# One matmul for the distance biases, split squares, and constant multiplications at the head of a decoder layer

## The reference, cut to what matters

```
mod = silu(c) @ w_ada + b_ada                  # w_ada: 2048 x 18432
sh1, sc1, g1, sh2, sc2, g2, sh3, sc3, g3 = split(mod, 9)
h = rms_norm(x, norm_ffn1) * (1 + sc1) + sh1
x = x + 0.5 * g1 * ((silu(h @ w1_gate) * (h @ w1_up)) @ w1_down)
...
s_w = q @ k * scale + rel_bias[t5_bucket(distance)]    # inside the token mixing
```

## Time and profile before

| | |
|---|---|
| three runs, median | 2060.33 us (2058.78 to 2060.92) |
| the profiled execution | 2060.54 us, its span 2058.7 us |
| TensorE busy | 2024.6 us, 98% of the span |
| VectorE, ScalarE busy | 1398.9 us (68%), 873.7 us (42%) |
| TensorE on the chain that ended last | 93% |
| mean transfer rate | 259 GB/s over the span |

### The profile page before, as it was taken

The page is one execution under the profiler, slowest core; times in us unless marked ns, Lnnn a source line. Parts: engine busy times, 40 slices in busy tenths (PEclk is TensorE's granted clock), DMA queues, the critical chain, the costliest instruction groups (busy, mean ns, idle before and its releaser), DMA issues.

```text
span 2058.7 us, 26899 instructions
## 1 busy us (share of the span) xinstructions
PE 2024.6 (98%) x9331; PEld 1605.0 (78%) x9331; DVE 1398.9 (68%) x1864; ACT 873.7 (42%) x1119; POOL 36.6 (2%) x56
## 2 busy tenths in 40 slices
PE   7999999999999999999999999999999999999998
PEld 4668888788888888787787888788888888888886
DVE  4557887877778889896556669777775545545454
ACT  3344434344443434543444644544444444434333
POOL 0000000000000000000005000000000000000000
PEclk9999999999999999999999999999999999999999
DMA  8998999799989889698967138589986777675654
GB/s 309 387 349 301 332 318 322 261 292 297 278 303 327 308 319 347 221 365 290 290 194 260 42 134 305 165 276 291 295 251 197 197 199 205 198 217 197 199 186 133
DMA packets 343366, 533.10 MB, mean 259 GB/s; under 512 B 80874, under 2 KB 99397, under 8 KB 342377
## 3 DMA queue, kind: packets, MB, share of 16 engines
q1 hardware_dynamic: 342648, 529.90, 77.6%
q10 hardware_dynamic: 624, 1.97, 0.3%
HBM read 520.04 MB, written 3.89 MB: 254 GB/s over the span
## 4 chain that ended last, share of the span: by engine, by line
PE 93%; DVE 2%; issue 1%; DMA 1%; ACT 1%; SPq 0%; ACTq 0%
PE ps L825 29%; PE ps L827 29%; PE ps L826 29%; PE ps L869 1%; PE ps L906 1%; DMA ada_half<-in_w_ada_dram 1%; PE ps L854 1%; DVE ada_acc L1941 1%; DVE w_lo L1923 1%; PE ps L1372 1%; PE ps L1375 1%; PE ps L1402 1%; PE ps L1207 0%; ACT w_hi L1496 0%; DMA raw<-in_w_uq_dram 0%
## 5 line engine op out<-in xcount | busy, mean ns | idle before, releaser
L1496 ACT ACTIVATE w_hi<-raw 128x1024 fp32r<-128x1024 f32 (+1 forms) x657 | 688.9, 1054 | 929.0 <-PE ps L827 552.6
L1923 DVE TENSOR_TENSOR w_lo<-raw,w_hi 128x1024 fp32r<-128x1024 f32 (+1 forms) x657 | 796.0, 1220 | 408.0 <-ACT w_hi L1496 402.4
L825 PE MATMUL ps<-w_hi,hT_hi 128*128 128x512 f32 (+1 forms) x1856 | 741.7, 400 | 6.5 <-DVE hT_lo L2058 4.3
L827 PE MATMUL ps<-w_hi,hT_lo 128*128 128x512 f32 (+1 forms) x1856 | 731.8, 394 | 0.0
L826 PE MATMUL ps<-w_lo,hT_hi 128*128 128x512 f32 (+1 forms) x1856 | 731.7, 394 | 0.0
L825 PEld LDWEIGHTS ps<-w_hi,hT_hi 128*128 128x128 f32 x1856 | 349.8, 188 | 102.4 <-issue 15.3
L827 PEld LDWEIGHTS ps<-w_hi,hT_lo 128*128 128x128 f32 x1856 | 349.8, 188 | 83.6
L826 PEld LDWEIGHTS ps<-w_lo,hT_hi 128*128 128x128 f32 x1856 | 350.1, 189 | 79.8 <-issue 0.5
L1941 DVE SCALAR_TENSOR_TENSOR ada_acc<-ada_raw,silu_c,ada_acc 128x512 f32<-128x512 f32 x420 | 315.4, 751 | 8.1
L825 PE MATMUL ps<-w_hi,actT_hi 128*128 128x512 f32 x704 | 280.0, 398 | 0.0
L827 PE MATMUL ps<-w_hi,actT_lo 128*128 128x512 f32 x704 | 279.1, 396 | 0.0
(11 more groups left out here) (245 smaller groups left out, 947.3 us busy)
## 6 DMA issues: line engine op xcount, KB each, us to landing
ada_raw<-in_w_ada_dram SPq DMA_DIRECT2D x224, 512.0 KB, 5.5
raw<-in_w_gate_dram SPq DMA_DIRECT2D x176, 512.0 KB, 4.9
raw<-in_w_up_dram SPq DMA_DIRECT2D x176, 512.0 KB, 4.9
raw<-in_w_down_dram SPq DMA_DIRECT2D x176, 512.0 KB, 5.0
raw<-in_w_in_dram SPq DMA_DIRECT2D x72, 512.0 KB, 5.8
ada_half<-in_w_ada_dram SPq DMA_DIRECT2D x14, 2048.0 KB, 12.9
raw<-in_w_out_dram SPq DMA_DIRECT2D x32, 512.0 KB, 5.4
actT_lo<-norm_tmp SPq DMA_DIRECT2D x240, 32.0 KB, 3.2
```

The source lines that it names most:

```text
L825: pe.matmul(bank, lhs_hi, rhs_hi, start=start, stop=False)
L827: return pe.matmul(bank, lhs_lo, rhs_hi, start=False, stop=stop)
L1496: act.activation(part(U, w_hi, s), part(U, raw, s), ACT.Copy).then_inc(hi_done, 1)
L1923: dve.tensor_tensor(part(U, w_lo, s), part(U, raw, s), part(U, w_hi, s).bitcast(F32), ALU.subtract)\
```

## The change

It has four parts. The nine bias matmuls become one: the table of 33 x 9 biases itself is the stationary operand, and the result has the nine rows on nine partitions. It runs after `turn_norm` 0, its scaled copy on VectorE after `first_low(0)`; `rel_rep` and its copy on GpSimd are gone. The store to memory now reads each of the nine rows 128 times, so that memory holds what it held before. The squares of `x` tile 1 are made by VectorE (`second_squares`), between the copy of `v_cols` and the mean, while ScalarE makes only those of tile 0; it also runs a Silu on a constant before them. And TensorE runs `keep_busy(n)`: n matmuls of the 128 x 128 tile of ones by itself into bank 0, whose result nothing reads; 28 before the transpose of `v_rows`, then 5, 12 and 6 at three later places.

```diff
--- before.py
+++ after.py
@@ -347,11 +347,12 @@
             bucket_sb = sb("bucket_sb", [BUCKETS + 1, 384], within=s)
             rel_sb = sb("rel_sb", [BUCKETS + 1, HEADS + 1], within=s)
             v_rows = sb("v_rows", [NV, P], within=s)
-            rel_rep = sb("rel_rep", [BUCKETS + 1, HEADS + 1, P], within=s)
+            behind_rel = sb("behind_rel", [P, (HEADS + 1) * P], within=s)
             silu_pad = sb("silu_pad", [P, KD, 32], within=s)
             ada_half = sb("ada_half", [P, HALF_RING, HALF * CW], within=s)
             behind_half = sb("behind_half", [P, 2240], within=s)
-            rev_b = sb("rev_b", [P, HEADS + 1, 384], within=s)
+            rev_b = sb("rev_b", [HEADS + 1, 384], within=s)
+            behind_rev = sb("behind_rev", [P, HEADS * 384], within=s)
             unshifted = sb("unshifted", [P, 2 * TT, CW], within=s)
         with ExitStack() as s:
             proj = sb("proj", [P, TT, D_IN], within=s)
@@ -511,10 +512,6 @@
         def blocked_before(f, u):
 
             return u + FF // CW - 1 - BLOCKS_FROM if f == 1 else u - BLOCKS_FROM
-
-        def bias_bank(h):
-
-            return T_BANK + 1 if h == HEADS else h % 4
 
         def ada_use(q, p):
 
@@ -758,10 +755,6 @@
             pool.memset(b_row[:, :, :], 0.0).then_inc(rows_set, 1)
             pool.memset(silu_pad[:, :, :], 0.0).then_inc(rows_set, 1)
             pool.memset(ones[:, :], 1.0).then_inc(rows_set, 1)
-            pool.wait_ge(rel_landed, 16 * 2)
-            pool.wait_ge(rel_set, 2)
-            pool.tensor_copy(rel_rep[:, :, :], rel_sb[:, :].unsqueeze(2).broadcast_to([BUCKETS + 1, HEADS + 1, P]))\
-                .then_inc(rows_set, 1)
 
             n_step = 0
 
@@ -859,8 +852,6 @@
                 q = i // 2
                 if i == 0:
                     pe.wait_ge(silu_c_done, 2)
-                if i == 2:
-                    pe.wait_ge(rev_done, HEADS + 1)
                 if i % 2 == 0 and q >= 2:
                     pe.wait_ge(acc_step, START_STEPS * (q - 1))
                 pe.wait_ge(half_landed[i % HALF_RING], 16 * (i // HALF_RING + 1))
@@ -1068,6 +1059,13 @@
                     last_panels(U, (act_hi, act_lo))
 
 
+            def keep_busy(n):
+
+                for _ in range(n):
+                    pe.matmul(ps[:, 0, 0:P], ones[:, :], ones[:, :], start=True, stop=True)
+
+            pe.wait_ge(rows_set, 3)
+            keep_busy(28)
             pe.wait_ge(const_landed, 16 * 7)
             pe.transpose(ps[:, MISC_BANK, 0:NV], v_rows[:, :], ident[0:NV, 0:NV]).then_inc(v_turned, 1)
 
@@ -1078,31 +1076,31 @@
 
                 u, j = i // 4, i % 4 * 4 + e
                 pe.wait_ge(nrm["ffn1"]["T_lo_done"], 2 * i + e // 2 + 1)
-                if j < 2 and u == 0:
-                    pe.wait_ge(rev_done, (6, 8)[j])
-                elif j < 2:
+                if (u, j) == (0, 1):
+                    pe.wait_ge(rev_done, 1)
+                elif u == 1 and j < 2:
                     pe.wait_ge(spilled, 2 * j + 2)
                 panel(Unit("gu0", u), j, (hT_hi, hT_lo), j // 2 * 2, 2 * (j % 2), j < 2, j >= KD - 2,
                       tile_ready=tile_ready)
 
-            def bias_rows(first, last):
-
-                for h in range(first, last):
-                    if 4 <= h < HEADS:
-                        pe.wait_ge(rev_done, h - 3)
-                    pe.matmul(ps[:, bias_bank(h), 0:384], rel_rep[:, h, :], bucket_sb[:, :], start=True, stop=True)\
-                        .then_inc(rev_mm, 1)
-
-            pe.wait_ge(rows_set, 4)
-            bias_rows(0, HEADS + 1)
+            def bias_rows():
+
+                pe.wait_ge(rel_set, 2)
+                pe.wait_ge(rel_landed, 16 * 2)
+                pe.matmul(ps[0:HEADS + 1, 3, 0:384], rel_sb[:, :], bucket_sb[:, :], start=True, stop=True)\
+                    .then_inc(rev_mm, 1)
+
+            keep_busy(5)
             start_part(0, 0)
-            pe.wait_ge(rows_set, 3)
+            keep_busy(12)
             spread_rstd("ffn1", T_BANK)
             start_part(0, 1)
             turn_part(0)
             pe.wait_ge(rstd_b_done, 1)
             turn_norm("ffn1", 0, x_tile)
+            bias_rows()
             start_part(1, 0)
+            keep_busy(6)
             for i in range(START_CHUNKS):
                 more, shift_next = i + 1 < START_CHUNKS, i + 1 >= LATE_SHIFT
                 turn_norm("ffn1", 2 * i + 1, x_tile)
@@ -1643,17 +1641,18 @@
             dma(pe_sb[:, 0:DK], pe_cmp_k[0]).then_inc(pe_landed, 16)
             dma(pe_sb[:, DK:DK + VD], pe_cmp_v[0]).then_inc(pe_landed, 16)
 
-            def first_squares(t):
-
-                act.wait_ge(x_landed[t], 16)
+            def first_squares():
+
+                act.wait_ge(x_landed[0], 16)
                 for c in range(D // CW):
-                    n = t * D // CW + c
-                    if n >= 2:
-                        act.wait_ge(nrm["ffn1"]["squares"], n - 1)
-                    act.activation(norm_tmp[:, c % 2, :], x_sb[:, t, c * CW:(c + 1) * CW], ACT.Square,
-                                   accum_out=x_sq[:, t, c:c + 1]).then_inc(nrm["ffn1"]["squares"], 1)
-
-            first_squares(0)
+                    if c >= 2:
+                        act.wait_ge(nrm["ffn1"]["squares"], c - 1)
+                    act.activation(norm_tmp[:, c % 2, :], x_sb[:, 0, c * CW:(c + 1) * CW], ACT.Square,
+                                   accum_out=x_sq[:, 0, c:c + 1]).then_inc(nrm["ffn1"]["squares"], 1)
+
+            act.wait_ge(rows_set, 3)
+            act.activation(stat[:, 5, 3:4], ones[:, 0:1], ACT.Silu)
+            first_squares()
             act.wait_ge(v_done, 1)
             act.activation(silu_c[:, :], v_cols[:, VROWS["c"]:NV], ACT.Silu).then_inc(silu_c_done, 1)
             act.wait_ge(rows_set, 2)
@@ -1714,9 +1713,7 @@
                         x_squares(("mix", "final")[f], res[U.stage]["x_added"], before(U))
 
 
-            act.wait_ge(rows_set, 3)
             load_root_table()
-            first_squares(1)
             root("ffn1", TT)
             copy_rstd("ffn1", T_BANK)
 
@@ -1741,8 +1738,9 @@
                 first_hi(2 * i + 1)
             for u in range(REDO, REDO + 2):
                 gate_up_unit(0, Unit("gu0", u))
-            act.wait_ge(rev_done, HEADS + 1)
-            dma(bias_scratch.ap(), rev_b[:, :, :]).then_inc(rev_stored, 16)
+            act.wait_ge(rev_done, 1)
+            dma(bias_scratch.ap().rearrange("p h n -> h p n"), rev_b[:, :].unsqueeze(1).broadcast_to([HEADS + 1, P, 384]))\
+                .then_inc(rev_stored, 16)
             for u in range(REDO + 2, REDO + 6):
                 gate_up_unit(0, Unit("gu0", u))
             for U in units(act, "gu0", REDO + 6, FF // CW):
@@ -1976,8 +1974,16 @@
                 then_wait(dve.tensor_scalar(e, e, -0.5, 1.5, ALU.mult, ALU.add))
                 then_wait(dve.tensor_tensor(out_, r, e, ALU.mult))
 
+            def second_squares():
+
+                dve.wait_ge(x_landed[1], 16)
+                for c in range(D // CW):
+                    xs = x_sb[:, 1, c * CW:(c + 1) * CW]
+                    then_wait(dve.tensor_tensor_reduce(act_sg[:, c % 2, :], xs, xs, 1.0, 0.0, ALU.mult, ALU.add,
+                                                       x_sq[:, 1, c:c + 1]))
+
             def x_rstd(n):
-                dve.wait_ge(nrm[n]["squares"], 2 * (D // CW))
+                dve.wait_ge(nrm[n]["squares"], D // CW)
                 then_wait(dve.tensor_reduce(stat[:, 0, 0:TT], x_sq[:, :, :], AX.X, ALU.add))
                 rstd(n, [(0, TT, D)])
 
@@ -2176,10 +2182,8 @@
 
             def copy_bias_rows():
 
-                for h in range(HEADS + 1):
-                    dve.wait_ge(rev_mm, h + 1)
-                    dve.tensor_scalar(rev_b[:, h, :], ps[:, bias_bank(h), 0:384], 1.0 / SCALE, None, ALU.mult)\
-                       .then_inc(rev_done, 1)
+                dve.wait_ge(rev_mm, 1)
+                dve.tensor_scalar(rev_b[:, :], ps[0:HEADS + 1, 3, 0:384], 1.0 / SCALE, None, ALU.mult).then_inc(rev_done, 1)
 
             def add_part(i):
 
@@ -2204,13 +2208,14 @@
                 then_wait(dve.scalar_tensor_tensor(scale_cols[:, 2 * i:2 * i + 2], mod_cols[:, c0:c0 + 2], 1.0,
                                                    v_cols[:, g0 + 2 * i:g0 + 2 * i + 2], ALU.add, ALU.mult))
 
-            copy_bias_rows()
+            second_squares()
             norm_x("ffn1")
             add_part(0)
             scale_part(0)
             first_tmp(0)
             start_lo(0, 0)
             first_low(0)
+            copy_bias_rows()
             start_lo(0, 1)
             add_part(1)
             scale_part(1)
```

## The result

| | before | after |
|---|---|---|
| median | 2060.11 us (2058.78 to 2061.26, 6 runs) | 2067.64 us (2065.82 to 2069.22, 6 runs) |
| the profiled execution | 2060.54 us, span 2058.7 | 2066.89 us, span 2065.0 |
| ratio to before | | 1.0037, 95% interval 1.0025 to 1.0050 |

The kernel became 7.5 us slower, where a gain of 8.7 was forecast. Two things lie in this number, and the profile after keeps them well apart.

A forecast was written before the change was run, and what follows sets the result against it. The nine bias matmuls bound the head, and their lateness left a hole in the transfers; 8.2 us by half 5 plus half a microsecond of VectorE waits made 8.7, 2060.54 to 2051.8, forecast 2051.6 us, range 2049.3 to 2056.5.

The forecast's parts named there:

- the hole in the transfers: Near 39 us, about 6 us without transfers, caused by the late head, which TensorE pays at 60 to 62.
- the sum: Start to half 5: first panel at 25, half 4 at 53.8, TensorE through half 5 at 57.4 instead of 65.60, 8.2 us.
- its last half microsecond: Third panel's stretch: about half a microsecond of VectorE waits that earlier `w_lo` can remove, putting the gain at 8.7.
- as taken from L869: Constant products in the head: clock rises as after L869's matmuls at 62.10, so the 28 end near 11 us.
- the slower rival: Head: clock isn't raised, the 28 end at 14.6, first panel 3.4 to 11.6 us later; 2063.7 to 2071.9; chance 0.12.
- a head up to 2 us slower costs nothing: At half 3: TensorE done with half 2 by 35, half 3 lands at 37.2, a margin of 2 us.
- The clock at half 3: Multiplying half 3: 1.8 us, or 3.5 if idle time of 2 to 3 us lets the clock fall; 3.5 taken.
- I cost it at nothing: panels lie ahead in four slots.: Store of the biases, near 240 us: reads 9 partitions instead of 128, costed at nothing because panels lie ahead.
- The second rival: Store of the biases on 9 of 16 DMA engines makes a panel late: gain 5.2, 2055.1 us; chance 0.10.
- at half 3's rate: Store of the biases: 1728 KB take 4.6 us on 16 engines, 8.1 on 9, so 3.5 us more.
- The rule of the Trainium skill cited with this rival: Bias store: engine count is the largest up to 16 dividing the outermost size of both sides, 9 here.
- The range: Whole kernel: 2049.3 to 2056.5 us, over the store and half of the hole, chance 0.83.

The follow-up runs named there:

- The versions without constants: The 51 multiplications of ones removed from the changed kernel: 2068.26 us; also removed with the bias rows stored once, then copied 128 times memory to memory: 2054.64 us.
- the run from memory: Changed kernel with the nine bias rows put in memory once, then copied from there, nine rows outermost, in 1536 byte packets: 2053.70 us, ratio 0.9970.
- the biases alone: Changed kernel without the ones multiplications, squares of both tiles on ScalarE, bias rows stored once then copied memory to memory with 128 copies outermost: 2053.45 us, ratio 0.9970.

## Why the prediction was wrong

*Where the gain comes from: right.* The nine bias matmuls and their copies were the head's bound, and the hole in the transfers was the price. The hole closed, the first panel came at 26.46 against 25 in the working, half 4 at 54.56 against 53.8, and half 5 was through at 58.2 against 57.4: 7.4 us where the sum had 8.2 before its last half microsecond. That correction was wrong: from the third panel to half 4 it took 54.56 - 40.88 = 13.68 us, not less than the 13.13 of before. And half 3 came at 39.0 instead of 37.2. The transfers ran at nearly the same rate, and the delay stood already at 22.50, where TensorE waits 1.78 us for a transfer of chunk 0 that the sum had without a wait; where it comes from was not tried.

*The clock: the right choice, of no weight.* The 28 products took 8.71 us and ended at 11.07, so the clock rose during them, as taken from L869, and the slower rival, that it stays low, was wrong. The forecast also said that a head up to 2 us slower costs nothing. The versions without constants show what that means: all that the constants can win ends in the wait for half 3. Nor did the constants keep the clock up: from 25 to 28 us, after that wait of 1.78 us, the granted clock was 0.59, and the first panel record took 0.78 us. The working put the constants into the sum of the head, but never asked whether the head would be late without them.

*The clock at half 3: wrong in size.* I took 3.5 us, it was 1.92 in the kernel after. What that won was lost with the later landing.

*The store: the step that failed.* "I cost it at nothing: panels lie ahead in four slots." The second rival had the place and half of the mechanism, a store on fewer engines that makes panels late, and I gave it 0.10. Its price of 3.5 us was worked out "at half 3's rate", that is with packets as fast as those of a load on 128 partitions. They took 0.18 us instead, since the nine neighbouring source partitions share a path, and the store over 30 us, longer than the lead of four slots, which held for about 24 us; then the wait, and half clock after it, cost 14.0 us (2067.64 against 2053.61). Had the working asked what a packet from a single partition costs, no row of before would have answered: no store of that kernel reads a few partitions many times. That is an unknown cost to be bounded from both sides, and the upper bound was taken from rows of another kind of transfer. The rule of the Trainium skill cited with this rival, on the count of engines (nine, as the packet counts bear out), pointed at the right instruction for a reason that the run from memory shows to cost nothing here.

*The range* ended at 2056.5, since no case in it combined the head's gain with a loss greater than it.

## What to carry to other kernels

A transfer costs not only its bytes and its engines but the narrowest place that its source is read through: 1.77 MB from nine neighbouring partitions took over 30 us and slowed the transfers behind it, while the same packets from memory, or from partitions four apart, cost TensorE nothing. When a change shrinks a tile from 128 partitions to a few, look at every transfer that reads it, also one far from the place of the change. And if a stage waits for a transfer that does not move, speeding up what comes before it gains nothing: ask first what is waited for once the change is in.

## What the runs showed that was not expected

Sixteen engines on one partition took 0.56 us for a packet, nine on nine neighbouring ones 0.18, nine on partitions four apart 0.067: more engines do not help where the partitions read are the limit.

TensorE's clock fell after some of the waits for half 3 and not after others, and not in the order of their lengths: after 2.98 us idle in the kernel after, and 1.94 in the biases alone, the 16 records took 1.92 us; after 4.40 idle they took 3.49, and before the change after a wait of 2.33 us, 3.50. At half 4 the kernel after and these two versions lie within 0.6 us of one another (54.33 to 54.90).
